# Key norms of the RWKV features: from one square, head sum, root and reciprocal per unit to one compact set per layer

## The chip, the cores and the metric

The kernel runs on one core of one Trainium2 chip. The metric is the device time of one execution in microseconds (us). A core has five engines that run their own queues in order and meet only at semaphores: TensorE (PE, matrix products into PSUM), VectorE (DVE), ScalarE (ACT, functions from tables), GpSimd (POOL) and SyncE (SP, which issues the DMAs here).

## The reference, cut to what matters

The kernel is one inference step of a two-layer decoder trunk (1024 prompt positions and 8 samples of 8 positions, 1088 in all). Each layer projects the normalised input once, into columns for an attention group (NSA) and an RWKV-7 group of 8 heads of 64. The change touches the keys of the RWKV group:

```python
xm = p_rw + (prev - p_rw) * p['rw_mu']
r, wa, k, v, aa, ga = jnp.split(xm, list(RW_SPLITS), axis=-1)
kk = heads(k * p['rw_k_k'])
kk = kk / jnp.maximum(jnp.sqrt(jnp.sum(kk * kk, axis=-1, keepdims=True)), 1e-12)
k_h = heads(k) * (1.0 + (a_h - 1.0) * k_a)
```

The sum runs over the 64 channels of a head, so there is one norm for each head and position: 8 x 1088 a layer. `kk`, times decays and gates, goes into the rows that the recurrence reads later.

## The kernel before, in words

For each layer, `projections` does the input projection in fp32, each product made of three products of high and low parts (`xh`, `xl`, `wh`, `wl`). Channels lie on the 128 partitions and positions on the free axis; the 1088 positions are cut into three groups of 384, 384 and 320 columns (`GROUPS`).

*Phase A.* Fourteen tiles of 128 RWKV channels, in the order `F_ORDER = (12, 0, 4, 1, 5, 2, 6, 3, 7, 8, 9, 10, 11, 13)`. Tile `f` from 4 to 7 holds the keys of two heads. TensorE makes 72 products for a tile (`rows_of`, L534). ScalarE copies them out of PSUM (L668 to L671), VectorE scales them and mixes them with the position before (L792 to L804), SyncE stores the tile to HBM (`X["xmT"]`, L411). The tiles alternate between two buffers and between PSUM banks 0 to 2 and 3 to 5. VectorE is a tile behind TensorE.

*Phase B.* Two things run interleaved in an order that `alternate` fixes for all engines: 45 NSA steps (five groups of columns, nine blocks of 128 positions each) and 12 feature units of four steps each. A unit is two heads (`hp`) in one group of columns (`grp`). The interleaving is about 3.6 NSA steps to a unit.

An NSA step: TensorE makes 24 products (L500), ScalarE copies the block to `kvt` (L598, or L603 and L604), VectorE rotates it in place (rope, L692 to L698), TensorE transposes the block of two steps before (L486), ScalarE copies that out (L579, L582). Three blocks are in flight.

A feature unit, by its steps:

- step 0: TensorE makes two lora products (L515, 64 rows each). ScalarE squares the keys times `rw_k_k` into `f_sq` (L623), writes the same product into `kk` (L624), and makes two sigmoids (L628, L629).
- step 1: TensorE sums the squares over each head, by a product with `cst["blk"]` that also spreads the sum over the 64 partitions of the head (L522). VectorE makes the running sum of decays (L714) and a difference (L716), ScalarE three exponentials (L635, L636, L638).
- step 2: VectorE bounds the sums from below (L719), makes `f_k2` (L723, L726), takes the reciprocal (L728) of ScalarE's root (L641). So guard, root and reciprocal are made on 128 partitions, of which 64 at a time hold the same number.
- step 3: VectorE normalises `kk` (L734) and makes the output rows (L740 to L752); GpSimd makes two products (L465, L467); SyncE stores them (L375, L376).

The keys of a unit are loaded back from HBM into `f_in` one unit ahead (`load_unit`, L333). ScalarE has one table of functions loaded at a time; sigmoid, exponential and root each need another, and a load (ACT_TABLE_LOAD) stands at the line of the function that needs it. The features' tiles (`work`) lie over the buffers of phase A, so all engines wait for `seed`, which SyncE sets when the last tile of phase A has been stored.

Of the kernel before, what the change touches and what calls it, by code (L numbers as in the profile page):

```python
# [242 lines left out]
def projections(nc, ps, cst, cbuf, ptab, carried, l, qT, ksT, kwT, vs, vw, gate, wend, A, O, X):  # L243
# [18 lines left out]
             "rk_in0 rk_in1 z_done gates_ready kk_ready sq_ready sq_done cum_ready prev_ready decays ak_ready maxed f_rooted recip_ready k_ready "  # L262
             "kkn_ready kka_ready read_k out_ready pool_out f_kept rk_kept vec1 seed")
    with Scope(nc) as sc, stage(nc, names) as (
# [3 lines left out]
            rk_in0, rk_in1, z_done, gates_ready, kk_ready, sq_ready, sq_done, cum_ready, prev_ready, decays, ak_ready, maxed, f_rooted, recip_ready, k_ready,  # L268
            kkn_ready, kka_ready, read_k, out_ready, pool_out, f_kept, rk_kept, vec1, seed):
# [25 lines left out]
        f_sw, f_cum, f_w, f_wi, f_pw, f_a0, f_a1, f_kk0, f_kk1, f_sq, f_tr = (work[:, n * U:(n + 1) * U] for n in range(11))  # L295
        f_a, f_kk = (f_a0, f_a1), (f_kk0, f_kk1)
        f_k2 = sc.sb("pr_k2", [P, U])
        f_rk = sc.sb("pr_rk", [P, U])
        f_in = sc.sb("pr_in", [P, 2, 2, U])
        f_out = sc.sb("pr_out", [P, 6, 4, CH])  # L300
        pieces = [(i, 0, KD) for i in range(nf)] + [(nf + n, k, 2) for n in range(len(NSA_GROUPS)) for k in range(0, KD, 2)]
# [59 lines left out]
        def features_sync(sp):  # L361
            for n, (hp, grp) in enumerate(UNITS):
                o, w = GROUPS[grp]
                if n + 1 < len(UNITS):
                    if n:
                        sp.wait_ge(read_k, n)
                        sp.wait_ge(pool_out, 2 * n)
                    load_unit(sp, n + 1)
# [137 lines left out]
        def features_tensor(pe):  # L506
            for n, (hp, grp) in enumerate(UNITS):
# [11 lines left out]
                pe.wait_ge(sq_ready, n + 1)  # L519
                if n:  # L520
                    pe.wait_ge(maxed, n)
                pe.matmul(ps[:, 7 * BANK:7 * BANK + w], cst["blk"], f_sq[:, 0:w], start=True, stop=True).then_inc(sq_done, 1)  # L522
# [5 lines left out]
        def _(pe):  # L528
# [27 lines left out]
            for i in range(2 if l == 0 else 0, nf):  # L556
                if i >= 2:
                    pe.wait_ge(raw_copied, i - 1)
                if i == (2 if l == 0 else 1):
                    pe.wait_ge(sums_read, 1)  # L560
                for k in range(KD):
# [47 lines left out]
        def features_scalar(act):  # L609
            for n, (hp, grp) in enumerate(UNITS):  # L610
                o, w = GROUPS[grp]
                a, kk = f_a[n % 2][:, 0:w], f_kk[n % 2][:, 0:w]
# [4 lines left out]
                else:  # L617
                    act.wait_ge(sq_done, n)
# [3 lines left out]
                act.wait_ge(rk_in[n % 2], 32 * (n // 2 + 1))  # L622
                act.activation(f_sq[:, 0:w], f_in[:, n % 2, 1, 0:w], ACT.Square, scale=vec[:, 2, hp:hp + 1]).then_inc(sq_ready, 1)  # L623
                act.activation(kk, f_in[:, n % 2, 1, 0:w], ACT.Copy, scale=vec[:, 2, hp:hp + 1]).then_inc(kk_ready, 1)  # L624
# [15 lines left out]
                act.wait_ge(maxed, n + 1)  # L640
# [2241 lines left out]
```

## Time and profile before

| | |
|---|---|
| median of the runs | 4388.35 us (4386.02 to 4398.71, 3 runs) |
| profiled execution, its own time | 4382.77 us |
| its span, first to last instruction | 4381.0 us |
| mean granted TensorE clock | 0.956 of full speed |
| busy share of the span: PE, DVE, ACT, POOL | 91%, 51%, 27%, 41% |
| phase B of layer 0 and of layer 1 | 214 us each |

Durations in the rows come from the profiled execution. Busy shares over the whole span say little here, as the change lies in the two projection stages; these are read by stretches of time. In a line of the trace an idle time in brackets is what the engine waited before the instruction, with the instruction that ended the wait. TensorE's instructions are pipelined: one lasts longer than the distance to the next.

### The profile page before, as it was taken

The page shows a single profiled execution, that of the slowest core. Times are in us where ns is not written, and L with a number is a line of the kernel's source. Part 1 is how long each engine was busy: PE and PEld are TensorE (multiplying, and loading weights), DVE is VectorE, ACT ScalarE, POOL GpSimd, SP SyncE. Part 2 cuts the span into 40 slices and gives each one's busy share as a digit, 9 for nine tenths or more (in the row PEclk, how much of TensorE's full clock was granted, in tenths as well). Part 3 has the DMA queues.
Part 4 walks back from the last instruction along what each step waited for, and adds up shares of the span by engine and source line. Part 5 has one row for each costly group of instructions (what it writes and reads, how often), then busy time and mean ns, then how long its engine had stood idle before and what let it go on. Part 6 is the DMA issues. An engine that isn't in the chain of part 4 may idle for free. (4 is left out here: it accounts for less than half of the span.)

```text
span 4381.0 us, 89581 instructions
## 1 busy us (share of the span) xinstructions
PE 3992.2 (91%) x36954; PEld 3643.2 (83%) x36954; DVE 2230.0 (51%) x4939; ACT 1179.9 (27%) x2557; POOL 1781.5 (41%) x2332
## 2 busy tenths in 40 slices
PE   8887899988789999999999778999788999999997
PEld 8876788875469999999898667888655799999996
DVE  5577543438754433414556765443587544234153
ACT  2155223326562000100212632332265510001011
POOL 5521311216765444434354322211277644444342
PEclk9998999988899999999999899999799999999998
DMA  3333522220003122131323343222200131221312
GB/s 115 99 120 96 166 68 75 78 91 25 13 20 130 44 77 93 45 120 52 105 87 99 119 159 101 79 80 62 91 6 12 49 107 47 96 74 44 126 44 87
DMA packets 201961, 350.43 MB, mean 80 GB/s; under 512 B 72930, under 2 KB 135650, under 8 KB 200418
## 3 DMA queue, kind: packets, MB, share of 16 engines
q1 hardware_dynamic: 201554, 344.70, 25.1%
q8 instruction: 293, 4.80, 0.5%
q14 instruction: 114, 0.93, 0.1%
HBM read 253.44 MB, written 95.90 MB: 80 GB/s over the span
## 5 line engine op out<-in xcount | busy, mean ns | idle before, releaser
L2541 POOL CAST wr_hi<-wr_raw 128x256 fp32r<-128x256 f32 x584 | 263.8, 452 | 905.5 <-PE ps L2576 899.6
L2543 POOL TENSOR_TENSOR wr_lo<-wr_raw,wr_hi 128x256 fp32r<-128x256 f32 x584 | 547.8, 938 | 46.7
L2576 PE MATMUL ps<-xh,wr_hi 128*128 128x384 f32 x2064 | 453.7, 328 | 0.0
L2576 PE MATMUL ps<-xl,wr_hi 128*128 128x384 f32 x2064 | 453.1, 327 | 0.0
L2576 PE MATMUL ps<-xh,wr_lo 128*128 128x384 f32 x2064 | 452.9, 327 | 0.0
L1317 POOL TENSOR_TENSOR rc_CT<-rc_AT,rc_masks 128x256 f32<-128x256 f32 x192 | 138.1, 738 | 661.9 <-DVE rc_AT L1352 482.7
L2576 PEld LDWEIGHTS ps<-xh,wr_lo 128*128 128x128 f32 x2064 | 349.0, 188 | 0.0
L2576 PEld LDWEIGHTS ps<-xh,wr_hi 128*128 128x128 f32 x2064 | 348.8, 188 | 0.3
L2576 PEld LDWEIGHTS ps<-xl,wr_hi 128*128 128x128 f32 x2064 | 348.9, 188 | 0.0
L2614 ACT ACTIVATE de_c<-de_c 128x1088 f32<-128x1088 f32 (+1 forms) x44 | 49.1, 1116 | 1098.1 <-DVE de_c L2701 1098.1
L2576 PE MATMUL ps<-de_mixh,wr_hi 128*128 128x384 f32 (+3 forms) x1440 | 321.4, 331 | 7.9 <-DVE de_mixl L2648 7.9
L2576 PE MATMUL ps<-de_mixl,wr_hi 128*128 128x384 f32 (+3 forms) x1440 | 318.9, 329 | 0.0
L2576 PE MATMUL ps<-de_mixh,wr_lo 128*128 128x384 f32 (+3 forms) x1440 | 317.8, 329 | 0.0
L2139 POOL TENSOR_TENSOR at_s<-at_s,at_fac 128x384 f32<-128x384 f32 (+3 forms) x320 | 255.8, 825 | 137.8 <-DVE at_fac L2122 137.2
L2662 DVE TENSOR_TENSOR de_x<-de_x,ps 128x384 f32<-128x384 f32 x168 | 79.3, 527 | 455.7 <-PE ps L2576 455.7
L1444 PE MATMUL ps<-sa_kt,cp_w 128*128 128x126 f32 x2304 | 295.2, 281 | 0.0
L1444 PEld LDWEIGHTS ps<-sa_kt,cp_w 128*128 128x128 f32 x2304 | 268.0, 191 | 9.7
L2576 PEld LDWEIGHTS ps<-de_mixh,wr_hi 128*128 128x128 f32 (+1 forms) x1440 | 246.0, 189 | 14.9 <-issue 14.9
L2576 PEld LDWEIGHTS ps<-de_mixh,wr_lo 128*128 128x128 f32 (+1 forms) x1440 | 247.9, 189 | 0.0
L2576 PEld LDWEIGHTS ps<-de_mixl,wr_hi 128*128 128x128 f32 (+1 forms) x1440 | 243.9, 188 | 0.0
L500 PE MATMUL ps<-pr_wh,xh 128*128 128x256 f32 (+1 forms) x720 | 226.3, 314 | 4.7 <-ACT pr_rsm L671 2.7
L500 PE MATMUL ps<-pr_wl,xh 128*128 128x256 f32 (+1 forms) x720 | 211.9, 294 | 0.0
(431 smaller groups left out, 8465.8 us busy)
## 6 DMA issues: line engine op xcount, KB each, us to landing
sa_kvp<-in_cache SPq DMA_DIRECT2D x128, 256.0 KB
scr_xres<-de_x SPq DMA_DIRECT2D x56, 544.0 KB, 2.7
de_x<-scr_xres SPq DMA_DIRECT2D x56, 544.0 KB, 3.6
wr_raw<-in_w_gate SPq DMA_DIRECT2D x42, 512.0 KB
wr_raw<-in_w_up SPq DMA_DIRECT2D x42, 512.0 KB
rc_arbk<-scr_arbk SPq DMA_DIRECT2D x32, 512.0 KB, 4.8
wr_raw<-in_w_down SPq DMA_DIRECT2D x32, 512.0 KB
pr_raw<-in_w_rw SPq DMA_DIRECT2D x28, 512.0 KB, 4.4
```

Source lines behind the costliest of these rows:

```text
L500: mm = pe.matmul(ps[0:m, b:b + w], x[:, k, t * P:t * P + m], weights(y, i)[:, k, :], start=(k == 0 and j == 0), stop=(k == KD - 1 and j == 2))
L1317: pool.tensor_tensor(CT[:, n % 2, s], AT[:, s], mid(lev[:, n * CH:(n + 1) * CH], 4), ALU.mult).then_inc(ct_ready[s], 1)
L1444: m = pe.matmul(ps[:, b:b + 126], w1[:, kv, q, half * P:(half + 1) * P], kt[:, 2 * kv:2 * kv + 2, q % 8, q // 8:q // 8 + 63], start=(q == ...
L2139: pool.tensor_tensor(x, x, fac[:, job % 6, g:g + 1].to_broadcast([P, w]), ALU.mult).then_inc(normed, 1)
L2541: pool.tensor_copy(hi[:, k, :], raw[:, k, :]).then_inc(w_hi, 1)
L2543: pool.tensor_tensor(lo[:, k, :], raw[:, k, :], f32(hi[:, k, :]), ALU.subtract).then_inc(w_ready, 1)
L2576: m = pe.matmul(ps[:, (bank + b) * BANK:(bank + b) * BANK + cols], w[rows, k, :], x[rows, k, o:o + cols], start=(k == 0 and i == 0), stop= ...
L2614: act.activation(c[rows, :], c[rows, :], ACT.Silu).then_inc(silu_done, 1)
L2662: m = dve.tensor_tensor(to[:, o:o + w], x[:, o:o + w], ps[:, (bank + b) * BANK:(bank + b) * BANK + w], ALU.add)
```

## The change

The norms are made once per layer in compact form, in 6 rows of partitions and not 128.

- Phase A: while key tile `q` is in its buffer, ScalarE squares it, times `rw_k_k`, into `sqk` (1088 columns, which lie over `f_out`). TensorE, two tiles later, sums it over the two heads with `pick`, a 128 x 32 matrix that is zero but for two columns of ones over one head each, shifted by 2 with the tile. Three such products cover the columns (`SPANS`, the third overlapping the second); they write 32 output partitions each, at partitions 0, 32 and 64 of PSUM bank 7, and are accumulated over the four tiles. So row `32 g + 2 q + h` holds head `h` of tile `q` in group `g`.
- On these 96 partitions and 384 columns VectorE applies the guard once (before tile 11), ScalarE the root once (after its copies of tile 12) and VectorE the reciprocal once (before tile 13, the last).
- Phase B: VectorE first builds `wide`, 8 rows at each of three partitions, which takes a head's row to the 64 partitions of the head. In place of the head sum TensorE makes the product of `wide` and `kr` (8 rows, 384 columns) into bank 7. VectorE multiplies keys, `rw_k_k` and this in one instruction that reads PSUM. Square, scaled copy, guard, root and reciprocal of the unit are gone. The spread of unit n waits for `kkn_ready` of unit n-1, and so does SyncE's load of the next unit.

```diff
@@ features_sync
-                        sp.wait_ge(read_k, n)
+                        sp.wait_ge(kkn_ready, n)
@@ features_tensor
-                pe.wait_ge(sq_ready, n + 1)
                 if n:
-                    pe.wait_ge(maxed, n)
-                pe.matmul(ps[:, 7 * BANK:7 * BANK + w], cst["blk"], f_sq[:, 0:w], start=True, stop=True).then_inc(sq_done, 1)
+                    pe.wait_ge(kkn_ready, n)
+                else:
+                    pe.wait_ge(picked, 5)
+                    pe.wait_ge(recip_ready, 1)
+                at, c0 = 32 * grp, o - SPANS[grp]
+                pe.matmul(ps[:, 7 * BANK:7 * BANK + w], wide[at:at + 8, hp * P:(hp + 1) * P],
+                          kr[at:at + 8, c0:c0 + w], start=True, stop=True).then_inc(spread, 1)
@@ tensor, before the products of tile i
+                if i - 3 in K_TILES:
+                    q = K_TILES.index(i - 3)
+                    pe.wait_ge(picked, 2)
+                    pe.wait_ge(sq_ready, q + 1)
+                    for g, at in enumerate(SPANS):
+                        m = pe.matmul(ps[32 * g:32 * g + 32, 7 * BANK:7 * BANK + 384], pick[:, 6 - 2 * q:38 - 2 * q], sqk[:, at:at + 384], start=(q == 0), stop=(q == 3))
+                    m.then_inc(sq_done, 1)
@@ features_scalar
-                    act.wait_ge(sq_done, n)
-                act.wait_ge(rk_in[n % 2], 32 * (n // 2 + 1))
-                act.activation(f_sq[:, 0:w], f_in[:, n % 2, 1, 0:w], ACT.Square, scale=vec[:, 2, hp:hp + 1]).then_inc(sq_ready, 1)
-                act.activation(kk, f_in[:, n % 2, 1, 0:w], ACT.Copy, scale=vec[:, 2, hp:hp + 1]).then_inc(kk_ready, 1)
...
-                act.wait_ge(maxed, n + 1)
-                act.activation(f_tr[:, 0:w], f_tr[:, 0:w], ACT.Sqrt).then_inc(f_rooted, 1)
@@ scalar, after the copies of tile i
+                if i - 1 in K_TILES:
+                    q = K_TILES.index(i - 1)
+                    act.wait_ge(in_misc, 96)
+                    act.wait_ge(mixed, i)
+                    if q:
+                        act.wait_ge(sq_done, q)
+                    act.activation(sqk, xm[:, (i - 1) % 2, :], ACT.Square, scale=vec[:, 2, q:q + 1]).then_inc(sq_ready, 1)
+                if i == nf - 2:
+                    act.wait_ge(guarded, 1)
+                    act.activation(kr[0:96, :], kr[0:96, :], ACT.Sqrt).then_inc(kr_rooted, 1)
@@ features_vector
+            dve.wait_ge(seed, 1)
+            for at in (0, 32, 64):
+                dve.tensor_copy(wide[at:at + 8, :].rearrange("p (h c) -> p h c", c=HD), bc(cst["ident"][at:at + 8, at:at + 8], HD)).then_inc(picked, 1)
...
-                dve.wait_ge(sq_done, n + 1)
-                dve.tensor_scalar(f_tr[:, 0:w], ps[:, 7 * BANK:7 * BANK + w], 1e-24, None, ALU.max).then_inc(maxed, 1)
...
-                dve.wait_ge(f_rooted, n + 1)
-                dve.reciprocal(f_tr[:, 0:w], f_tr[:, 0:w]).then_inc(recip_ready, 1)
...
-                dve.sem_inc(read_k, 1)
-                dve.wait_ge(recip_ready, n + 1)
-                dve.wait_ge(kk_ready, n + 1)
-                dve.tensor_tensor(kk, kk, f_tr[:, 0:w], ALU.mult).then_inc(kkn_ready, 1)
+                dve.wait_ge(spread, n + 1)
+                dve.scalar_tensor_tensor(out=kk, in0=k_in, scalar=vec[:, 2, hp:hp + 1], in1=ps[:, 7 * BANK:7 * BANK + w], op0=ALU.mult, op1=ALU.mult).then_inc(kkn_ready, 1)
@@ vector, phase A
+            dve.memset(pick[:, :], 0.0).then_inc(picked, 1)
...
+            dve.tensor_copy(pick[:, 6:8], cst["blk"][:, 63:65]).then_inc(picked, 1)
...
+                if i == nf - 3:
+                    dve.wait_ge(sq_done, 4)
+                    dve.tensor_scalar(kr[0:96, :], ps[0:96, 7 * BANK:7 * BANK + U], 1e-24, None, ALU.max).then_inc(guarded, 1)
+                if i == nf - 1:
+                    dve.wait_ge(kr_rooted, 1)
+                    dve.reciprocal(kr[0:96, :], kr[0:96, :]).then_inc(recip_ready, 1)
+                if i - 2 in K_TILES:
+                    dve.wait_ge(sq_ready, K_TILES.index(i - 2) + 1)
```

## Rows read from the trace of the kernel before

**Rows 1.** Windows: phase A, between, phase B (layer 0); phase B (layer 1).

```profile
core 0: us, PE busy (x) PEld busy (x) DVE busy (x) ACT busy (x) POOL busy (x), PEclk, DMA share, GB/s
77.00:197.00 120.00, 120.00 (x721) 119.75 (x719) 62.60 (x90) 14.94 (x42) 68.70 (x77) 1.00 0.28 94
197.00:214.00 17.00, 4.28 (x29) 3.29 (x28) 11.37 (x15) 2.21 (x6) 12.11 (x10) 0.76 0.47 116
214.00:428.00 214.00, 169.89 (x1178) 152.80 (x1178) 166.90 (x436) 125.21 (x242) 48.28 (x50) 0.91 0.34 103
...
2375.00:2589.00 214.00, 168.99 (x1178) 151.16 (x1178) 168.09 (x436) 125.04 (x241) 48.12 (x50) 0.91 0.34 104
```

**Rows 2.** Waits of TensorE and VectorE, 214 to 428 us: total, times, longest.

```profile
PE ps L486 <- DVE pr_kvt L698: 36.3, 20, 6.3
...
DVE pr_tb L692 <- ACT pr_kvt L604: 21.0, 5, 5.2
DVE pr_tb L692 <- ACT pr_kvt L598: 15.7, 6, 3.1
```

**Rows 3.** Timeline in a unit of layer 0: start, length, engine, line.

```profile
266.28 0.95 DVE L714 TENSOR_TENSOR_SCAN pr_work<-pr_restart,pr_work 128x384 f32<-128x384 f32 x1
...
270.51 0.22 DVE L692 TENSOR_TENSOR pr_tb<-pr_kvt,pr_cs 128x64 f32<-128x64 f32 x1 [2.70 <-ACT pr_kvt L604]
...
271.45 0.55 DVE L719 TENSOR_SCALAR pr_work<-ps 128x384 f32<-128x384 f32 x1
...
272.90 2.55 DVE L728 RECIPROCAL pr_work<-pr_work 128x384 f32<-128x384 f32 x1
...
273.19 0.36 ACT L604 ACTIVATE pr_kvt<-ps,pr_rs 128x128 f32<-128x128 f32 x1
```

**Rows 4.** Groups by line, 214 to 428 us: busy, mean ns, idle before.

```profile
L728 DVE RECIPROCAL pr_work<-pr_work 128x384 f32<-128x384 f32 (+1 forms) x12 | 29.0, 2413 | 2.6 <-ACT pr_work L641 2.6
...
L641 ACT ACT_TABLE_LOAD x12 | 15.4, 1283 | 0.2
...
L623 ACT ACTIVATE pr_work<-pr_in,pr_vec 128x384 f32<-128x384 f32 (+1 forms) x12 | 7.4, 616 | 10.2 <-DMA pr_in<-scr_xmT 10.2
...
L641 ACT ACTIVATE pr_work<-pr_work 128x384 f32<-128x384 f32 (+1 forms) x12 | 6.1, 507 | 2.9 <-DVE pr_work L719 2.5
```

**Rows 5.** Timeline, layer 0: head sums (L522) and key products (L734).

```profile
277.57 0.55 DVE L734 TENSOR_TENSOR pr_work<-pr_work 128x384 f32<-128x384 f32 x1
277.87 0.49 PE L522 MATMUL ps<-pr_work,cbuf 128*128 128x384 f32 x1
...
293.47 0.59 PE L522 MATMUL ps<-pr_work,cbuf 128*128 128x384 f32 x1 [1.87 <-ACT pr_work L623]
...
298.74 0.54 DVE L734 TENSOR_TENSOR pr_work<-pr_work 128x384 f32<-128x384 f32 x1
```

**Rows 6.** Timeline, layer 0: a lora pair and a head sum on TensorE.

```profile
239.28 0.92 PE L515 MATMUL ps<-pr_wa,pr_lora 64*128 64x384 f32 x4
...
318.17 0.82 PE L522 MATMUL ps<-pr_work,cbuf 128*128 128x384 f32 x2
```

**Rows 7.** Timeline, layer 1, phase A: one tile to the next.

```profile
2349.19 0.48 ACT L668 COPY pr_work<-ps 128x384 f32<-128x384 f32 x1 [10.75 <-PE ps L534]
...
2350.48 1.89 DVE L792 TENSOR_TENSOR pr_work<-pr_work,rs 128x1024 f32<-128x1024 f32 x1 [5.68 <-ACT pr_rsm L671]
...
2361.20 0.48 ACT L668 COPY pr_work<-ps 128x384 f32<-128x384 f32 x1 [10.75 <-PE ps L534]
```

**Rows 8.** Timeline between the phases, layer 0 and layer 1.

```profile
210.27 1.31 SPq L333 DMA_DIRECT2D pr_in<-scr_xmT  x2
...
213.52 0.61 ACT L623 ACTIVATE pr_work<-pr_in,pr_vec 128x384 f32<-128x384 f32 x1 [10.16 <-DMA pr_in<-scr_xmT]
...
216.56 0.96 DVE L714 TENSOR_TENSOR_SCAN pr_work<-pr_restart,pr_work 128x384 f32<-128x384 f32 x1 [6.58 <-ACT pr_work L628]
...
2373.68 1.30 SPq L333 DMA_DIRECT2D pr_in<-scr_xmT  x2
...
2377.86 0.96 DVE L714 TENSOR_TENSOR_SCAN pr_work<-pr_restart,pr_work 128x384 f32<-128x384 f32 x1 [3.76 <-ACT pr_work L628]
```

More of the change, by code:

```diff
@@ L261, in projections @@
              "n_done n_copied n_turned n_kept ta_done rotated gates_made kv_kept0 kv_kept1 kv_kept2 "
-             "rk_in0 rk_in1 z_done gates_ready kk_ready sq_ready sq_done cum_ready prev_ready decays ak_ready maxed f_rooted recip_ready k_ready "
-             "kkn_ready kka_ready read_k out_ready pool_out f_kept rk_kept vec1 seed")
+             "rk_in0 rk_in1 z_done gates_ready picked sq_ready sq_done spread cum_ready prev_ready decays ak_ready guarded kr_rooted recip_ready k_ready "
+             "kkn_ready kka_ready out_ready pool_out f_kept rk_kept vec1 seed")
     with Scope(nc) as sc, stage(nc, names) as (
@@ L267, in projections @@
             n_done, n_copied, n_turned, n_kept, ta_done, rotated, gates_made, kv_kept0, kv_kept1, kv_kept2,
-            rk_in0, rk_in1, z_done, gates_ready, kk_ready, sq_ready, sq_done, cum_ready, prev_ready, decays, ak_ready, maxed, f_rooted, recip_ready, k_ready,
-            kkn_ready, kka_ready, read_k, out_ready, pool_out, f_kept, rk_kept, vec1, seed):
+            rk_in0, rk_in1, z_done, gates_ready, picked, sq_ready, sq_done, spread, cum_ready, prev_ready, decays, ak_ready, guarded, kr_rooted, recip_ready, k_ready,
+            kkn_ready, kka_ready, out_ready, pool_out, f_kept, rk_kept, vec1, seed):
         x_in, w_in, sent, kv_kept, rk_in = (x_in0, x_in1), (w_in0, w_in1, w_in2), (sent0, sent1), (kv_kept0, kv_kept1, kv_kept2), (rk_in0, rk_in1)
@@ L294, in projections @@
         U = 384
-        f_sw, f_cum, f_w, f_wi, f_pw, f_a0, f_a1, f_kk0, f_kk1, f_sq, f_tr = (work[:, n * U:(n + 1) * U] for n in range(11))
+        f_sw, f_cum, f_w, f_wi, f_pw, f_a0, f_a1, f_kk0, f_kk1, f_rk = (work[:, n * U:(n + 1) * U] for n in range(10))
         f_a, f_kk = (f_a0, f_a1), (f_kk0, f_kk1)
         f_k2 = sc.sb("pr_k2", [P, U])
-        f_rk = sc.sb("pr_rk", [P, U])
+        kr = sc.sb("pr_kr", [P, U])
+        pick = sc.sb("pr_pick", [P, 38])
+        wide = work[:, 10 * U:10 * U + 4 * P]
         f_in = sc.sb("pr_in", [P, 2, 2, U])
         f_out = sc.sb("pr_out", [P, 6, 4, CH])
+        sqk = f_out[:, :, :, :].rearrange("p c a t -> p (c a t)")[:, 0:NT]
+        K_TILES = [F_ORDER.index(hp + 4) for hp in range(4)]
+        SPANS = (0, 384, NT - 384)
         pieces = [(i, 0, KD) for i in range(nf)] + [(nf + n, k, 2) for n in range(len(NSA_GROUPS)) for k in range(0, KD, 2)]
@@ L611, in features_scalar @@
                 o, w = GROUPS[grp]
-                a, kk = f_a[n % 2][:, 0:w], f_kk[n % 2][:, 0:w]
+                a = f_a[n % 2][:, 0:w]
                 if n == 0:
@@ L778, in _ @@
             dve.memset(raw[:, :, 0:1], 0.0)
+            if l == 0:
+                dve.wait_ge(const_in, 32)
+            dve.wait_ge(picked, 1)
+            dve.tensor_copy(pick[:, 6:8], cst["blk"][:, 63:65]).then_inc(picked, 1)
             dve.wait_ge(in_misc, 96)
```

## The prediction

> **What bounds the kernel now.** I read the stretches of the windows view first [rows 1], because the change touches only the stage of the projections, which runs once per layer. The reader is to see three stretches in each layer. While the 14 RWKV tiles are made (phase A) TensorE is busy for all of the time, at the full clock, and VectorE for 52%. Then come some 15 us in which TensorE does almost nothing (layer 0: 4.3 us busy of 17). Then come 214 us (phase B, 45 NSA steps with 12 feature units between them) in which TensorE, VectorE and ScalarE are busy 79%, 78% and 59%. So phase A is worth what TensorE's instructions cost, and in phase B no engine is the limit by itself.
>
> The waits of phase B say how it goes [rows 2]. In layer 0 TensorE's transposes wait 36.3 us for VectorE's rope, and VectorE waits 21.0 and 15.7 us, together 37, for ScalarE's copies. TensorE runs at most three NSA steps ahead, so its waits for the rope are VectorE's lateness, handed on. VectorE's own time is about 167 of 214 us, plus 37 us in which ScalarE holds it up; TensorE's is about 169. The long chain of phase B is therefore VectorE's work and, after each scan, ScalarE's table load, three exponentials and copy [rows 3]: the scan starts at 266.28, the next rope can't start before 270.51, and VectorE idles 2.70 us.
>
> **Phase B: what goes.** On VectorE each unit loses the guard (L719) and the reciprocal (L728). L728 took 2.41 us in the mean [rows 4] and L719 0.55 with its end [rows 3]; instructions of this size on VectorE overlap a little, so I count 0.5 for it: 0.5+2.41 = 2.9 us a unit, 12x2.9 = 35 us a layer. The product L734 (0.55 [rows 5]) becomes one with three operands, one of them in PSUM. No row shows that form. I bound it at 0.5 and 0.6, a tenth around L734, which over 12 units is 0.6 us either way; L719, which reads PSUM with the same 384 columns, took the same 0.55 [rows 3], so I add nothing. The VectorE page of the Trainium skill ("VectorE: DVE Perf Modes", the TRN2 errata) says otherwise: a PSUM source has a fixed cost of 120 cycles against 58. By it each unit would lose 0.065 us and the forecast 0.8 us a layer; the two rows of this trace at equal size speak against it.
>
> On ScalarE each unit loses the square, the scaled copy, the load for the root (1.28) and the root (0.51). The square took 0.62 [rows 4] and the copy has its size, with some overlap 1.1 for both; together it is about 2.9 us a unit, 35 us a layer. The loads for the sigmoid and the exponential stay. This work stood between VectorE's guard and the next copies to the ropes, so it frees the same chain, and it isn't to be added to VectorE's 35.
>
> On TensorE the spread product has the columns of the head-sum product it replaces, so it costs the same.
>
> If VectorE's 35 us went in full, phase B would take 179 us. TensorE needs 169 by its busy row, so it just allows it. But two engines whose paces are that near, coupled by three buffers, wait for each other now and then. Some reciprocals also hide a wait: the one at 272.90 ends 2.55 us later, while the copy for the next rope ends at 273.55 [rows 3], so that at once only 1.9 of 2.5 is won there. I take four fifths: **28 us a layer**; the bounds are 15 (only what those spots show at once, about 1.3 a unit) and 38 (35, and some of TensorE's 45 idle microseconds, with a better clock than the 0.91 of [rows 1]).
>
> **Phase B: what is added.** The spread of unit n waits until VectorE has normalised the keys of unit n-1, where the head sum waited for ScalarE's square. Behind it in TensorE's queue stand the next NSA step and the next lora products, and for these ScalarE and VectorE. By the old times it is nearly free: the head sum of a unit started at 277.87 where L734 of the unit before began at 277.57 [rows 5], since both stand behind the same rope. One of the eleven would have waited long: the head sum at 293.47 against an L734 at 298.74, 5.8 us [rows 5]. There VectorE is late, which is what shrinks. I count nothing; a rival has it in full. SyncE loads the next unit's keys when that product is done and not just before it, about 0.5 us later; the load runs a unit (some 15 us) ahead of use and hides in it.
>
> **Phase A: what is added.** TensorE gets 12 fp32 products of 384 columns a layer (four tiles, three spans), each with 32 output partitions. A head sum of 384 columns took 0.82 us [rows 6]. One after another they are at most 4x3x0.82 = 10 us a layer. If the three strips, which lie on different output partitions, overlap wholly, they are 4x0.82 = 3.3 us. The nearest row is the pair of lora products on the two halves of the rows: 0.92 us for two products of 384 columns [rows 6], where 1.64 would be due, so the second added 0.1. I take 1.25 us a tile, nearer to this row than to the upper bound, **5 us a layer**, and nothing of it hides, because tile follows tile every 12.00 us [rows 7] with TensorE full. The page "TensorE: Matmul & The Clock Gate" of the Trainium skill (Packing small matmuls) gives a speedup of 2.38 for three column tiles; by it the sum would be 10/2.38 = 4.1 us a layer instead of 5. No row here shows column tiles.
>
> The rest of phase A has cover. The squares (1088 columns, so at most three of the 0.62 of L623) stand in 10.75 us of idle time of ScalarE, the guard in 5.68 us of VectorE [rows 7], the root with its load (1.8) in ScalarE's again. TensorE asks for a tile's square two tiles after it was copied out, some 24 us, and it is there after about 14. Two tiny instructions ahead of VectorE's long reciprocal in each layer lie in a stretch in which TensorE multiplies tiles on.
>
> **Between the phases.** The compact reciprocal (384 columns, 2.55) is put in front of VectorE's work on the last tile, and that work is the path: its result is stored, the features are released when the store has landed (SyncE's next loads at 210.27), ScalarE starts at 213.52 when the keys are in, and VectorE's scan at 216.56 [rows 8]. With the change the release comes 2.55 later, at 212.8. But ScalarE then has no square and waits for no keys: load 1.28 and sigmoid 0.6, and the scan starts at 214.7 instead of 216.56, 1.8 earlier. In layer 1 SyncE's loads and the scan are at 2373.68 and 2377.86 [rows 8]; the release would be at 2376.2, the scan at 2378.1, 0.3 later. VectorE's three small copies into the spreading matrix lie beside ScalarE's load (512 columns each; between nothing and three times the 0.55 of L719, 1.7 us in all, and the load and sigmoid cover 1.9). Together 1.5 us is won.
>
> **The sum.** 2x28 won, 2x5 lost, 1.5 won: 47.5 us. Against the profiled execution's own 4382.77 this is 4335; against the median of the runs, 4388.35, it is **4341 us**, and since the profiled one was 5.6 us faster than the median, I name 4339. A difference under 0.3% (13 us) I take for what a measurement here can't tell from no change.
>
> **Rivals.**
> 1. *ScalarE and TensorE set the pace.* The time of the reciprocal turns into a wait for the copies; for it speaks the copy at 273.55 and that VectorE already waits 37 us a layer for ScalarE; against it, that ScalarE loses as much. Then 15 us a layer: 2x15-10+1.5 = 21.5 won, 4365; with the strips one after another (10 a layer) as well, 4375.
> 2. *Nearly all comes through,* with less idling and less of the lowered clock: 2x38-2x3+1.5 = 71 won, 4316.
> 3. *The new wait takes over: slower.* Each spread waits for the key product as the one at 293.47 would, 5.8 us, 12x5.8 = 70 us of idle TensorE a layer, where its whole idle time in phase B is 45. Phase B would take 169+70 = 239 instead of 214, and with phase A 2x(25+5)-1.5 = 58 lost, 4445. It decides from about (45-5)/12 = 3.3 us a unit on. Against it stands the pair at 277, like which the other units look, and that VectorE is less late after the change.
> 4. *The change doesn't act:* phase B is held by what it leaves alone (scan, exponentials, copies), and wins nothing: 2x5-1.5 = 8.5 lost, 4395. Against it, VectorE's waits for ScalarE are 37 us while its busy time is 167.
>
> **Chances.** Forecast (4325 to 4355) 0.55; rival 1 0.2; rival 2 0.14; rival 3 0.05; rival 4 0.06. The range that reaches to rivals 1 and 2 is 4316 to 4372; the forecast's own range is 4325 to 4355. Faster by more than 13 us: the forecast, rival 2 and most of rival 1, 0.85. Within it 0.09, slower 0.06.
>
> **What the profile after would show.** No lines for guard, root and reciprocal in phase B; 24 table loads fewer; phase B about 186 us long, VectorE's busy time in it near 134 and TensorE's share over 85%; waits of the spread product on VectorE in sum under 10 us a layer. In phase A four tiles of each layer 13.2 us apart and not 12.0. The scan of unit 0 1.8 us nearer to the last copy of phase A in layer 0. I am wrong if VectorE's waits for the copies before the ropes grow by what the reciprocal gave up, or if the spread product waits some microseconds in every unit.

## The result, and the profile after

The changed kernel took 4366.32 us in the median of four runs (4362.95 to 4369.65), the kernel before 4391.06 us in the median of four: ratio 0.9941, 95% interval 0.9928 to 0.9954, so 24.7 us or 0.6% faster. The forecast was 4339 us: the sign is right and the time lies in the range (4316 to 4372), but only half of the gain came. Rival 1 had priced 4365; its mechanism was another than the one found below.

The profiled executions are closer together (4382.77 and 4364.07 us, spans 4381.0 and 4362.3). I split their 18.7 us at points that both traces show: the first NSA product of phase B, its last transpose, and the ends of the stages behind it.

| stage | before ends at | after ends at | change |
|---|---|---|---|
| layer 0, phase A | 198.4 | 202.0 | +3.6 |
| layer 0, gap and phase B | 427.2 | 413.9 | -16.9 |
| layer 0, recurrence | 964.0 | 953.6 | +2.9 |
| layer 0, the rest, to layer 1's norm sums | 2191.5 | 2181.1 | 0.0 |
| layer 1, phase A | 2362.5 | 2356.9 | +4.8 |
| layer 1, gap and phase B | 2588.9 | 2570.5 | -12.8 |
| the rest | 4347.5 | 4328.6 | -0.5 |

The windows view of the kernel after, with the columns of [rows 1]. Here phase B is cut from the first scan to the last transpose: 197.3 and 198.5 us. The same cut of before is 216.6 to 427.6 and 2377.9 to 2589.2, 211.0 and 211.4 us.

```profile
77.00:201.00 124.00, 123.63 (x743) 119.95 (x742) 62.89 (x91) 21.32 (x49) 68.83 (x76) 1.00 0.27 91
...
216.90:414.20 197.30, 171.61 (x1178) 150.38 (x1178) 149.88 (x412) 86.88 (x187) 50.64 (x50) 0.92 0.36 113
2372.10:2570.60 198.50, 173.26 (x1178) 152.17 (x1178) 150.39 (x413) 87.33 (x187) 51.56 (x50) 0.91 0.36 112
```

The windows view of the kernel before, on that cut of layer 0:

```profile
216.60:427.60 211.00, 167.48 (x1173) 150.99 (x1172) 166.86 (x436) 122.39 (x238) 48.28 (x50) 0.92 0.33 102
```

Phase B is 13.7 us shorter in layer 0 and 12.9 in layer 1. TensorE's granted clock in it is the same (0.92 and 0.91 of the full 2.4 GHz, before 0.92 in both layers), so the missing half of the gain isn't the clock's. ScalarE's busy time fell by 35.5, as forecast. VectorE's fell from 166.9 to 149.9, which is 17 us, though the guard (6.3) and the reciprocals (29.0 [rows 4]) are gone. So 16 to 18 us came back (16 by the sum of the groups, 18 by the busy time) in instructions most of which the diff doesn't touch. The groups by line show where; after, VectorE in 216.90 to 414.20 (busy us, mean ns, idle before):

```profile
L714 DVE TENSOR_TENSOR pr_tb<-pr_kvt,pr_cs 128x64 f32<-128x64 f32 (+3 forms) x44 | 17.6, 399 | 0.0
L715 DVE TENSOR_TENSOR pr_tb<-pr_kvt,pr_cs 128x64 f32<-128x64 f32 (+3 forms) x44 | 17.3, 393 | 0.0
L757 DVE TENSOR_TENSOR pr_out<-pr_k,pr_work 64x384 f32<-64x384 f32 (+1 forms) x24 | 17.1, 712 | 0.2
...
L712 DVE TENSOR_TENSOR pr_tb<-pr_kvt,pr_cs 128x64 f32<-128x64 f32 (+3 forms) x44 | 12.2, 278 | 44.0 <-ACT pr_kvt L620 21.2 <-ACT pr_kvt L614 21.1 <-DVE pr_kvt L718 0.5
...
L759 DVE SCALAR_TENSOR_TENSOR pr_out<-pr_work 128x384 f32<-128x384 f32 (+1 forms) x12 | 9.5, 794 | 0.2
...
L751 DVE SCALAR_TENSOR_TENSOR pr_work<-pr_in,pr_vec,ps 128x384 f32<-128x384 f32 (+1 forms) x12 | 7.0, 584 | 0.0
```

The same view of the kernel before, VectorE in 216.60 to 427.60, the same statements under their old lines:

```profile
L694 DVE TENSOR_TENSOR pr_tb<-pr_kvt,pr_cs 128x64 f32<-128x64 f32 (+3 forms) x44 | 14.0, 318 | 0.0
L740 DVE TENSOR_TENSOR pr_out<-pr_k,pr_work 64x384 f32<-64x384 f32 (+1 forms) x24 | 13.7, 572 | 0.2
L695 DVE TENSOR_TENSOR pr_tb<-pr_kvt,pr_cs 128x64 f32<-128x64 f32 (+3 forms) x44 | 13.1, 299 | 0.0
...
L742 DVE SCALAR_TENSOR_TENSOR pr_out<-pr_work 128x384 f32<-128x384 f32 (+1 forms) x12 | 6.4, 537 | 0.2
...
L734 DVE TENSOR_TENSOR pr_work<-pr_work 128x384 f32<-128x384 f32 (+1 forms) x12 | 6.3, 528 | 0.0
```

The two middle rope products (L694, L695, now L714, L715) cost 7.8 us more with the same shapes and counts, the pair L757 3.4 and L759 3.1 (794 ns in the mean against 537). A busy row is thus no property of the instruction alone. What ran beside them shows in the timeline of the kernel before, at a reciprocal:

```profile
292.11 0.56 DVE L726 TENSOR_TENSOR pr_k<-pr_k,pr_in 128x384 f32<-128x384 f32 x1
...
292.59 2.54 DVE L728 RECIPROCAL pr_work<-pr_work 128x384 f32<-128x384 f32 x1
...
292.81 0.99 POOL L465 TENSOR_TENSOR pr_rk<-pr_in,pr_k 128x384 f32<-128x384 f32 x1 [15.90 <-DVE pr_k L726]
...
293.76 1.00 POOL L467 TENSOR_TENSOR pr_out<-pr_in,pr_work 128x384 f32<-128x384 f32 x1
```

and in the timeline of the kernel after, at the same place of a unit:

```profile
288.06 0.56 DVE L747 TENSOR_TENSOR pr_k<-pr_k,pr_in 128x384 f32<-128x384 f32 x1
...
288.75 1.01 POOL L470 TENSOR_TENSOR pr_work<-pr_in,pr_k 128x384 f32<-128x384 f32 x1 [13.03 <-DVE pr_k L747]
...
289.02 0.82 DVE L712 TENSOR_TENSOR pr_tb<-pr_kvt,pr_cs 64x64 f32<-64x64 f32 x1 [0.41 <-ACT pr_kvt L620]
...
289.72 0.99 POOL L472 TENSOR_TENSOR pr_out<-pr_in,pr_work 128x384 f32<-128x384 f32 x1
289.77 1.02 DVE L713 TENSOR_TENSOR pr_tb<-pr_kvt,pr_cs 64x64 f32<-64x64 f32 x1
290.66 0.61 POOL L448 CAST pr_wh<-pr_raw 128x512 fp32r<-128x512 f32 x1
...
290.72 0.62 DVE L714 TENSOR_TENSOR pr_tb<-pr_kvt,pr_cs 64x64 f32<-64x64 f32 x1
...
291.35 1.26 POOL L450 TENSOR_TENSOR pr_wl<-pr_raw,pr_wh 128x512 fp32r<-128x512 f32 x1
...
291.51 1.18 DVE L717 TENSOR_TENSOR pr_kvt<-pr_tb 64x64 f32<-64x64 f32 x1
...
293.17 0.60 DVE L751 SCALAR_TENSOR_TENSOR pr_work<-pr_in,pr_vec,ps 128x384 f32<-128x384 f32 x1
293.25 1.26 POOL L450 TENSOR_TENSOR pr_wl<-pr_raw,pr_wh 128x512 fp32r<-128x512 f32 x1
...
293.82 0.99 PE L530 MATMUL ps<-pr_kr,pr_work 8*128 8x384 f32 x2 [4.37 <-DVE pr_work L751]
```

In both kernels GpSimd's two products of a unit start when VectorE's product with the keys (L726, now L747) is done: 0.14 us after its end before (292.81), 0.13 after (288.75). Before, the reciprocal stood there for 2.5 us, and all three kept their length. After, VectorE goes straight to the rope, and its small instructions, for which [rows 3] have 0.22 us, last until a GpSimd instruction ends: 0.82, 1.02, 0.62, 1.18. The reader is to see what the slowed ones of these rows have in common: they read two tiles in SBUF. L751 reads one of its two from PSUM and takes 0.60 beside a GpSimd instruction of 1.26; the reciprocal reads one tile. But one tile alone is no safeguard. Elsewhere in the timeline of the kernel after, a copy of six columns that takes 0.16 us with no GpSimd instruction beside it took 1.25:

```profile
348.49 1.48 POOL L450 TENSOR_TENSOR pr_wl<-pr_raw,pr_wh 128x512 fp32r<-128x512 f32 x1
...
348.74 1.25 DVE L762 COPY wend<-pr_work 128x6 f32<-128x6 f32 x1
```

The product of one tile with scalars (L744) took 0.90 once, beside GpSimd, and 0.47 otherwise. The Trainium skill, "SBUF — State Buffer", on its two sides, says that VectorE and GpSimd share a pair of ports, and that the pair belongs for a whole instruction to whichever starts first: a GpSimd instruction, or one of VectorE that has two SBUF inputs or runs in a two-port mode. These rows agree with it, the last two on the condition that the copy and L744 run in such a mode, which no run here shows. The page spoke against counting VectorE's 35 us in full, and my prediction didn't weigh it.

The waits of the kernel after, 216 to 415 us, against [rows 2]:

```profile
PE ps L491 <- DVE pr_kvt L718: 17.5, 13, 4.3
...
PE ps L530 <- DVE pr_work L751: 7.9, 5, 4.4
PE ps L530 <- DVE pr_work L724: 7.6, 1, 7.6
```

One line of the waits view of the kernel before, 214 to 428 us, belongs beside [rows 2], the head sum's own waits:

```profile
PE ps L522 <- ACT pr_work L623: 17.7, 5, 10.6
```

TensorE's waits for the rope fell from 36.3 to 17.5. The spread product waits 15.5 us (7.9 and 7.6) where the head sum waited 17.7, so its waits are not an addition in layer 0; in layer 1 they are 18.5 against 13.5. VectorE's idle time before the ropes rose from 38 to 44.

### The profile page after: what moved, and what is told of

Read it like the earlier page. It is cut to its first block and busy times, and to the rows that moved or that the text cites. A ratio compares the mean times of both kernels' runs of the same rounds, so it can differ in the third digit from the quotient of the medians.

```text
span 4362.3 us, 89496 instructions
## 1 busy us (share of the span) xinstructions
PE 4005.4 (92%) x37002; PEld 3642.2 (83%) x37002; DVE 2200.8 (50%) x4905; ACT 1121.2 (26%) x2467; POOL 1792.6 (41%) x2332
```

## The experiments

Two theories stood against each other. **G**: the reciprocal was cover for GpSimd; without it GpSimd's products and weight splits meet VectorE's instructions with two SBUF inputs, and the two take turns. **S**: phase B is held by the waits between the engines (ScalarE's copies before the ropes, the spread's new wait), and VectorE's saved time turns into waiting whatever GpSimd does. The "slowing" in the expectations is the time of VectorE's instructions in a phase B beyond what the same line and shape takes with no GpSimd instruction beside it. Summed over the trace's instructions of layer 0 it is 15 us in the kernel before and 29 in the changed one. Phase B below is from the first scan to the last transpose in layers 0 and 1, with VectorE's busy time in it, both from the windows view.

| kernel | median, us | ratio to before | phase B | VectorE busy |
|---|---|---|---|---|
| changed kernel | 4366.32 | 0.9941 (0.9928 to 0.9954) | 197.3, 198.5 | 149.9, 150.4 |
| before_no_pool | 4377.77 | 0.9972 (0.9963 to 0.9982) | 203.1, 205.2 | 160.3, 161.9 |
| after_no_pool | 4327.54 | 0.9870 (0.9845 to 0.9894) | 182.5, 183.1 | 137.4, 137.4 |
| before_no_recip | 4380.57 | 0.9971 (0.9960 to 0.9982) | 204.9, 205.2 | 155.5, 157.5 |
| after_dummy_recip | 4383.86 | 0.9983 (0.9972 to 0.9993) | 205.2, 207.5 | 164.0, 164.5 |
| two_input | 4416.71 | 1.0060 (1.0043 to 1.0077) | 225.3, 223.5 | 181.2, 181.7 |
| early_w | 4352.91 | 0.9912 (0.9895 to 0.9930) | 190.3, 189.4 | 144.6, 143.9 |
| early_w_rk_vector | 4342.37 | 0.9892 (0.9878 to 0.9906) | 187.3, 187.0 | 141.3, 141.9 |
| before_cured | 4392.38 | 1.0001 (0.9991 to 1.0011) | 210.0, 212.2 | 166.7, 168.3 |
| spread_late | 4358.58 | 0.9919 (0.9906 to 0.9932) | 195.2, 194.7 | 152.1, 150.3 |
| act_root | 4373.38 | 0.9958 (0.9943 to 0.9974) | 200.5, 200.8 | 146.2, 148.6 |
| both_late | 4338.27 | 0.9873 (0.9857 to 0.9890) | 184.5, 185.1 | 142.3, 141.7 |

The kernel before took 4392.40 us beside the first group of four below, 4389.37 beside the second, 4393.19 beside both_late, before_cured and one_strip, and 4388.52 beside two_input. The changed kernel wasn't run again beside the later groups. So its difference from another kernel is taken twice below: by the medians, and by the ratios to the kernel before of the same group, which is the safer of the two.

**GpSimd's products left out, in both kernels** (before_no_pool, after_no_pool): they are made in unit 0 alone.

```diff
+                    if n:
+                        pool.sem_inc(pool_out, 1)
+                        pool.wait_ge(decays, 3 * n + 1)
+                        pool.sem_inc(pool_out, 1)
+                        yield
+                        continue
                     pool.tensor_tensor(f_rk[:, 0:w], f_in[:, n % 2, 0, 0:w], f_k2[:, 0:w], ALU.mult).then_inc(pool_out, 1)
```

> The kernel before, with GpSimd's two feature products made for unit 0 alone (so the stored rows of the other units are wrong). Theory G (the reciprocal was cover for GpSimd): in the kernel before these products ran beside the reciprocal and slowed VectorE's other instructions by 1.2 us a layer only, so the time falls by 0 to 5 us, to about 4388. Theory S (ScalarE's copies and TensorE set the pace after the change): about the same, 4388. This run is the reference point for the next one.

> The changed kernel, with GpSimd's two feature products made for unit 0 alone (stored rows of the other units are wrong). Theory G: in the changed kernel they slow VectorE's instructions beside them by 14 to 15 us a layer, so the time falls by 22 to 30 us, from 4366 to about 4340, and phase B from 198 to about 185 us. Theory S: VectorE's freed time turns into waits for ScalarE's copies; the time falls by less than 8 us and those waits grow from 43 to about 55 us a layer.

By the ratios the products cost the kernel before 12 us and the changed one 31 (by the medians 14.6 and 38.8). So the change is worth 26 us with them and 45 without (by the medians 24.7 and 50.2): without these 22 GpSimd instructions a layer it gains about what I had forecast. Both costs are above G's expectation (0 to 5 and 22 to 30), so the cover in the kernel before was only partial. In its timeline the reciprocals of layer 0 lie over 19.5 of the 23.1 us of the two products. The slowing of VectorE fell from 15 to 8 us in the kernel before and from 29 to 17 in the changed one. Even without the products phase B shrinks by 21 to 22 us a layer and VectorE's busy time by 23 to 24.5, not 35. The weight splits L448 and L450 still run; the reciprocals had lain over 5.7 of their 26.3 us. The windows view of after_no_pool, with the columns of [rows 1]:

```profile
214.40:396.90 182.50, 167.25 (x1178) 148.07 (x1178) 137.37 (x412) 86.73 (x187) 28.37 (x28) 0.95 0.39 122
```

TensorE is busy for 92% of it: what is left is near its own work.

**The reciprocal alone, taken away and put back.** In before_no_recip the kernel before loses only L728 (the root is scaled by 1e-8 and the keys are multiplied by it, so they aren't normalised). In after_dummy_recip the changed kernel gets a reciprocal of another tile at the old place, whose result nobody reads.

```diff
 before_no_recip
-                dve.reciprocal(f_tr[:, 0:w], f_tr[:, 0:w]).then_inc(recip_ready, 1)
+                dve.sem_inc(recip_ready, 1)
 after_dummy_recip
                 dve.tensor_tensor(f_k2[:, 0:w], f_k2[:, 0:w], k_in, ALU.mult).then_inc(k_ready, 1)
+                dve.reciprocal(rs[:, 0:w], a)
```

> The kernel before without the reciprocal of each unit (keys are multiplied with a scaled root and not divided by it), all else unchanged: square, head sum, guard and root stay. It takes 58 us of VectorE's work away. Theory G: GpSimd's products and weight splits then fall on other VectorE instructions, whose slowing rises from 15 to 28 or more us a layer; the time falls by 25 to 32 us, to about 4362. Theory S: the slowing stays at 15 us a layer, and the waits for ScalarE's copies rise from 37 to over 50 us a layer; the time falls by a similar 25 us.

> The changed kernel with one reciprocal of the unit's size put back where the old one stood in VectorE's queue, its result unused. It adds 58 us of VectorE's work. Theory G: the slowing of VectorE's other instructions falls back from 29 to about 15 us a layer, so the time rises by 25 to 32 us only, to about 4394. Theory S: the slowing stays at 29 and the waits for copies shrink by what the reciprocal takes.

58 us of reciprocals left the kernel before and 11.8 us of time with them (13 by the ratio); both theories had said 25 or more. The slowing rose to 30 us, as G had said, and the waits for ScalarE's copies from 37 to 44, about half of the way to the 50 that S had named. Put into the changed kernel the reciprocals cost 17.5 us (4383.86 against 4366.32, or 18 by the ratios), where G had said 25 to 32, and the slowing fell to 17. The groups by line of after_dummy_recip, VectorE, 216 to 425 us, show why it is so little:

```profile
L748 DVE RECIPROCAL rs<-pr_work 128x384 f32<-128x384 f32 (+1 forms) x12 | 28.9, 2412 | 0.0
...
L758 DVE TENSOR_TENSOR pr_out<-pr_k,pr_work 64x384 f32<-64x384 f32 (+1 forms) x24 | 14.0, 585 | 0.2
...
L760 DVE SCALAR_TENSOR_TENSOR pr_out<-pr_work 128x384 f32<-128x384 f32 (+1 forms) x12 | 6.4, 536 | 0.2
```

The pair is back at 585 ns (from 712) and the three-operand product at 536 (from 794), near their times before. 29 us of work came in, and VectorE's busy time rose by only 14. TensorE's granted clock in phase B fell too, from 0.92 to 0.88 (0.87 in two_input below), so that a part of these two kernels' time may be the clock's; no run parts the two.

**Is it the length or the kind?** In two_input two instructions with two SBUF inputs stand where the reciprocal stood, planned to fill a similar time. If any long instruction shelters GpSimd, it should end near after_dummy_recip; by G it gives no shelter.

```diff
                 dve.tensor_tensor(f_k2[:, 0:w], f_k2[:, 0:w], k_in, ALU.mult).then_inc(k_ready, 1)
+                for e in range(2):
+                    dve.tensor_tensor(rs[:, :], f32(xh[:, 0, :]), f32(xh[:, 1, :]), ALU.max).then_inc(picked, 1)
+                    dve.wait_ge(picked, 6 + 2 * n + e)
```

> The changed kernel with two VectorE instructions put where the old reciprocal stood, each of 1088 columns with two inputs from SBUF (about 1.2 us each, 2.4 us a unit like the reciprocal), results unused. Theory G with the port as its mechanism (an instruction with two SBUF inputs and a GpSimd instruction take turns, one with a single input and GpSimd's run side by side): no cover, the slowing of 29 us a layer stays and the 29 us of added work come on top; phase B grows by about 16 to 20 us a layer and the time to about 4400. If any long VectorE instruction covers GpSimd's products (a matter of their place in time, not of the inputs): as after_dummy_recip, 4384.

It took 4416.71 us, slower than the kernel before. The group by line, VectorE, 216 to 445 us:

```profile
L749 DVE TENSOR_TENSOR rs<-xh 128x1088 f32<-128x1088 f32 x24 | 39.4, 1643 | 0.4
```

The pair is 3.3 us a unit and not 2.4, since these instructions are hit themselves: single ones took from 1277 to 2373 ns. GpSimd's busy time in phase B rose from 50.6 to 72.6 us for the same 50 instructions. So it isn't the length that covers, and a long instruction of this kind delays GpSimd as well. The time went further up than G had said; the sign and the kind are as it said.

**The cure.** If G holds, moving GpSimd's two products into time in which VectorE idles must win in the changed kernel and nothing before, where they had cover. In early_w the product with the decay moves to behind the first exponential, when VectorE waits for ScalarE; in early_w_rk_vector VectorE makes the other product itself; before_cured is the same cure in the kernel before.

```diff
 early_w (GpSimd; the guard of VectorE waits for 2 * n instead of 2 * n - 1)
                     yield
-                    yield
-                    yield
                     pool.wait_ge(rk_in[n % 2], 32 * (n // 2 + 1))
+                    pool.wait_ge(decays, 3 * n + 1)
+                    if n:
+                        pool.wait_ge(f_kept, 16 * n)
+                    pool.tensor_tensor(f_out[:, 0:w // CH, 1, :], ...).then_inc(pool_out, 1)
+                    yield
+                    yield
                     pool.wait_ge(k_ready, n + 1)
 early_w_rk_vector and before_cured, as well (VectorE, ahead of the normalised key)
+                if n:
+                    dve.wait_ge(rk_kept, 16 * n)
+                dve.tensor_tensor(f_rk[:, 0:w], f_in[:, n % 2, 0, 0:w], f_k2[:, 0:w], ALU.mult).then_inc(pool_out, 1)
```

> The changed kernel, full computation; GpSimd makes the product of receptance and decay as soon as ScalarE's first exponential is ready and no longer after the keys. Most of it then lies in the 2 to 5 us in which VectorE waits after the scan for ScalarE. Theory G (GpSimd's products collide with VectorE's): one of the two products stops colliding, the slowing of VectorE's instructions falls from 29 to about 22 us a layer and the time by 10 to 14 us, to about 4353. Theory S (ScalarE and TensorE set the pace): no change within 4 us.

> As early_w, full computation, and VectorE itself makes the other product (0.56 us a unit more of its own work). Theory G: neither product collides; against early_w VectorE gains about 7 us of slowing a layer and pays 12x0.56 = 6.7, so the time is that of early_w within 4 us, while the slowing falls to about 15 to 17 us a layer. Theory S: VectorE's work is not what counts, so again no change, within 4 us of 4366.

> The kernel before, full computation, with the cure of early_w_rk_vector alone (one GpSimd product early, the other on VectorE). Theory G: there the reciprocal already hides both products, so the slowing of VectorE's instructions stays at about 15 us a layer and VectorE pays 6.7 us a layer more of its own work: 4390 to 4402, no gain. Theory S or a general gain from less GpSimd work: as much as in the changed kernel, 24 us, 4366.

Against the changed kernel early_w won 13.4 us by the medians (13 by the ratios, whose intervals just touch) and early_w_rk_vector 24.0 (21.5 by the ratios, clear of the interval). The latter gives VectorE 12 more instructions a layer; its busy time fell all the same, from 149.9 to 141.3. The slowing fell from 29 to 24 and 16 us. early_w is where G had put it; early_w_rk_vector is 9 to 10 us below it, where I had said the same within 4, though their intervals overlap. In the kernel before the same edit is worth nothing (1.0001): its slowing fell from 15 to 10 us, and VectorE's own product costs 6.7. The cure pays only where the cover is gone.

**S's two parts.** In act_root ScalarE gets a root with its table load back in each unit (result unused); in spread_late the spread product stands one feature step later in TensorE's queue.

```diff
 act_root
                 yield
+                act.wait_ge(gates_ready, 2 * n + 2)
+                act.activation(rs[:, 0:w], a, ACT.Sqrt)
                 yield
 spread_late
                 m.then_inc(z_done, 1)
                 yield
+                yield
                 if n:
                     pe.wait_ge(kkn_ready, n)
...
-                yield
                 yield
                 yield
```

> The changed kernel with a root (and so its table load, 1.28 us, and 0.5 us) put back on ScalarE in each unit where the old one stood, its result unused. It adds 12x1.8 = 21 us of ScalarE's work a layer, just before the copies that the ropes wait for. Theory S (ScalarE sets the pace): nearly all of it shows, 30 to 43 us in the two layers, 4400. Theory G: ScalarE has slack at that place except where VectorE is already waiting; 8 to 20 us, about 4380.

> The changed kernel, full computation; TensorE makes the spread product one feature step (about 0.9 NSA steps) later, when the key product of the unit before is long done. If the added wait (7.9 us of TensorE's idle time a layer in the changed kernel) cost what it shows, the time falls by up to 16 us, to 4350. If TensorE has slack there, as Theory G says for a VectorE-bound phase, the wait moves to the transposes behind it and the time stays within 4 us of 4366.

act_root took 7.1 us more than the changed kernel (7.5 by the ratios), for 24 us of ScalarE's time a layer (busy 86.9 to 110.9), just under G's 8 to 20 and far from S's 30 to 43. The intervals of the two ratios overlap, so S's share isn't told from nothing; at some 7 us it is the smaller one beside the 21 to 24 that moving GpSimd's products is worth. The square and the scaled copy were not put back. spread_late took 7.7 us less (10 by the ratios), more than G's 4, but here too the intervals touch. The waits of TensorE in it, 216 to 413 us:

```profile
PE ps L491 <- DVE pr_kvt L718: 26.3, 12, 4.3
PE ps L531 <- DVE pr_work L724: 3.1, 1, 3.1
PE ps L531 <- DVE pr_work L751: 0.6, 2, 0.4
```

The spread's waits went from 15.5 to 3.7 us, and 8.8 of these 11.8 came back before the transposes: TensorE waits for VectorE either way.

**Both.** both_late joins early_w_rk_vector and spread_late and computes all that the reference asks.

> early_w_rk_vector and spread_late together, full computation. If the two act on different waits, their gains (24 and 8 us against the changed kernel) add up to about 4335; if spread_late won its 8 us only by moving VectorE's and GpSimd's instructions against each other, it wins nothing more here and the time is 4342 within 4 us.

4338.27 us, ratio 0.9873: 4 us below early_w_rk_vector by the medians and 8 by the ratios, with intervals that overlap, so that it isn't settled whether spread_late's gain adds in full. It is the fastest full version, 1.27% below the kernel before where the change alone gives 0.59%.

**Phase A: three strips or one.** In one_strip three more head-sum products per key tile are issued, all onto one strip of output partitions; nobody reads them.

```diff
                     m.then_inc(sq_done, 1)
+                    for g, at in enumerate(SPANS):
+                        pe.matmul(ps[96:128, 7 * BANK:7 * BANK + 384], pick[:, 6 - 2 * q:38 - 2 * q], sqk[:, at:at + 384], start=True, stop=True)
```

> The changed kernel with three more products of the same size behind each tile's three in phase A, all on one strip of output partitions (96 to 127) and unused. The three on different strips lengthen a key tile's period from 12.00 to 12.98 us. If only different strips overlap, the three on one strip cost 3 times 0.65 = about 2 us, and the period is near 15 us; if the place of the strip doesn't matter, it is near 14.

One run took 4383.31 us; what counts is the period of the tile. The timeline of one_strip, layer 1, at one key tile (L575: the kernel's three products, L578: the added ones):

```profile
2258.50 0.52 PE L575 MATMUL ps<-pr_out,pr_pick 128*32 128x384 f32 x3
2258.52 0.51 PE L578 MATMUL ps<-pr_out,pr_pick 128*32 128x384 f32 x1
...
2258.61 0.48 ACT L680 COPY pr_work<-ps 128x384 f32<-128x384 f32 x1 [7.23 <-PE ps L543]
...
2258.85 0.50 PE L575 MATMUL ps<-pr_out,pr_pick 128*32 128x384 f32 x3
2258.87 1.78 PE L578 MATMUL ps<-pr_out,pr_pick 128*32 128x384 f32 x5
...
2272.88 0.48 ACT L680 COPY pr_work<-ps 128x384 f32<-128x384 f32 x1 [13.01 <-PE ps L543]
```

Each product is two passes. The first pass of all four strips starts within 0.02 us, the second 0.35 later. The three products on three strips are over 0.85 us after the first began (2259.35), the three on one strip 2.15 us after (2260.65): their six passes follow one another. A key tile takes 14.27 us from copy to copy (2272.88 - 2258.61), against 12.97 in the changed kernel (next section); the 1.30 more are the difference of 2.15 and 0.85. The period lies nearer to the 14 of the other theory than to the 15 that I had expected, since I had put the added products behind the kernel's three and their first two passes run beside these. So the period alone doesn't decide; the starts do: products on one strip add up and products on different strips run side by side.

## Why the prediction was right in sign and half in size

**The step that failed: "35 us of VectorE a layer".** The removed lines were worth what I had read (6.3 + 29.0). The term was wrong because I took the durations of all the other instructions as fixed. VectorE's gain was 17.0 us in layer 0 and 17.7 in layer 1. The runs showed in its place: the reciprocal was cover for GpSimd's work, and with it gone 18 of the 35 us came back as longer VectorE instructions. That is most of what is missing, since by the ratios the change wins 45 us without GpSimd's products and 26 with them. Which instruction a long one shelters stood in the rows around L728, and I hadn't looked at GpSimd's.

**The four fifths** that I let come through look right in layer 0 (0.8 x 17.0 = 13.6, against 13.7 measured), but that is luck. It was 12.9 of 17.7 in layer 1, and 20.6 of 22.9 between the two kernels without GpSimd's products. That the time came to rival 1's price of 4365 is luck as well: it stood for a VectorE that waits for the copies in the reciprocal's time, and that wait grew by 6 and 8 us in the two layers, not by 35. Of the signs that I had named, TensorE's share came (87%), but phase B is 197 us long and not 186, and VectorE's busy time 150 and not 134.

**ScalarE's 35 us** were right (35.5); 24 of them, the root and its load, were worth some 7 us by act_root, with the doubt said there. Of its table loads 15 a layer went in phase B and not 12 (38 to 23), as three of the others were no longer needed in the new order. Phase A has one more for the compact root, so the whole kernel has 28 fewer (130 to 102) and not 24.

**The spread's wait, counted as nothing:** its own waits were 15.5 us in layer 0 and 18.5 in layer 1 where I had said under 10, with 7.6 and 10.2 of it at unit 0, for the three copies into the spreading matrix. The head sum's 17.7 and 13.5 went, which I hadn't listed, so that from nothing to 5 us a layer were added. The long wait that I had found at one place in eleven is there (4.37 at 293.82); the other four share 3.5. Most of it is TensorE's wait for VectorE under another name: moved, it reappears before the transposes. Rival 3 is out: behind unit 0 no spread wait was longer than 4.4, and in each layer only 6 of 12 waited.

**L734 with a PSUM operand, counted at no extra:** 584 ns against 528, so 0.056 us a unit and 0.7 a layer. The Trainium skill's figure ("VectorE: DVE Perf Modes", errata), 0.065, which I had set aside, was the better one. I had set it aside by comparing L719 (PSUM, 0.55) with a product of two tiles; its like with an SBUF source, L723, took 0.47 in the same trace (at 291.61).

**Phase A, +5 a layer:** ScalarE's first copies of three tiles running, layer 1 of the changed kernel, in the timeline:

```profile
2318.63 0.48 ACT L678 COPY pr_work<-ps 128x384 f32<-128x384 f32 x1 [9.63 <-PE ps L543]
...
2331.60 0.48 ACT L678 COPY pr_work<-ps 128x384 f32<-128x384 f32 x1 [11.72 <-PE ps L543]
...
2343.60 0.48 ACT L678 COPY pr_work<-ps 128x384 f32<-128x384 f32 x1 [10.75 <-PE ps L543]
```

A key tile takes 12.97 us, the next 12.00 as in [rows 7]: 0.97 a tile, 3.9 a layer (my 1.25 and 5 were a little high). "TensorE: Matmul & The Clock Gate" of the Trainium skill, with its 2.38 for three column tiles, gave 4.1, and the trace agrees. Layer 1's phase A grew by 4.8, the other 0.9 being a wait at its start for GpSimd's weight split. The squares, the guard and the root hid, as forecast. (The compact set fills 24 rows, eight heads in each of three groups, of the 96 partitions.)

**Between the phases, layer 0:** the scan of unit 0 came 3.3 us nearer to phase A, where I had said 1.8. The timeline of the kernel after:

```profile
209.37 1.28 ACT L640 ACT_TABLE_LOAD   x1 [0.39 <-PE ps L520]
...
215.15 0.58 ACT L640 ACTIVATE pr_work<-ps,pr_vec 128x384 f32<-128x384 f32 x1 [4.49 <-SPq L423]
...
215.53 1.31 DVE L724 COPY pr_work<-cbuf 8x512 f32<-8x512 f32 x3
...
216.87 0.96 DVE L737 TENSOR_TENSOR_SCAN pr_work<-pr_restart,pr_work 128x384 f32<-128x384 f32 x1
```

ScalarE loads its table before it waits, so the load that I had put on the path isn't on it. The three small copies (1.3 us) are, as they stand ahead of the scan. In layer 1 the distance didn't change (I had 0.3 later).

**After phase B** I had expected nothing. 2.9 us of layer 0's gain and 0.9 of layer 1's were given back in the recurrence stage, whose code is the same. In the traces of the 14 kernels of this document, which all share that code, the stage took 533 to 543 us in layer 0 and 539 to 547 in layer 1, without an order by kernel. So these differences lie within what one execution differs from another, and aren't shown to come from the change. Open is how much of spread_late's gain both_late keeps.

In sum, by the profiled executions: phase B 26.6 won (I had 56), phase A 8.4 lost (10), the gap in layer 0 3.3 won (1.5 in both), 3.8 given back behind: 17.7 of the 18.7 us. These are single executions, and a stage of theirs can be off by some us, as the recurrence shows.

## What to carry to other kernels

A duration in a profile holds for the neighbours that it was measured beside. Before a long VectorE instruction is removed, look at what GpSimd does under it: if it runs beside GpSimd undisturbed, as the reciprocal did, and what follows reads two tiles from SBUF, its time is partly shelter, and some of the gain is lost until GpSimd's work is moved under another wait. A 2x2 of runs (the edit, and GpSimd's work left out, each with and without the other) tells this in one go; here it read 26 us and 45 us. And judge a removed instruction by how the engine's whole busy time falls, not by its own line.

## What the runs showed of the hardware that I had not expected

- A VectorE instruction with two SBUF inputs and a GpSimd instruction take turns: a 64x64 product that takes 0.22 us alone took 0.62 to 1.18 beside GpSimd instructions of 0.61 to 1.26. The delay goes both ways: GpSimd's 50 instructions of phase B took 72.6 us instead of 50.6 beside 24 long ones of VectorE.
- Two SBUF inputs aren't the only case: a VectorE copy of 128x6 from one tile took 1.25 us beside a GpSimd instruction of 1.48, and 0.16 with none beside it.
- VectorE's fp32 reciprocal doesn't do this: GpSimd's products beside it took 0.99 and 1.00 us, and it 2.54; all eight of 384 columns in layer 0 took 2.54 or 2.55. Nor does an instruction whose second input is in PSUM (L751, 0.60 beside GpSimd's 1.26; in layer 0 the four of 384 columns beside GpSimd instructions took 0.60 in the mean, the four others 0.61).
- An fp32 head-sum product of 384 columns is two passes of about 0.33 us; passes onto four different strips of output partitions started within 0.02 us of each other, and those on one strip followed one another.
- ScalarE's table load runs ahead of the wait of the instruction that needs it: at 209.37, for a sigmoid that started at 215.15.
